# Experts of a mixture layer: tokens stationary instead of weights, spare rows as fp32 products on four column groups

## What is computed

```python
def grouped_moe(x, router_w, router_bias, w1, w3, w2):
    ...
    _, top_idx = lax.top_k(masked_sel, TOP_K)          # 2 of 16 experts, within one group of 4
    ...
    for e in range(N_EXPERTS):
        h = jax.nn.silu(t @ w1[e]) * (t @ w3[e])       # 1024 -> 512, twice
        y = y + gate[:, e:e + 1] * (h @ w2[e])         # 512 -> 1024
    return y.reshape(Bsz, S, D)
```

## Time and profile before

| | us |
|---|---|
| median of 3 runs | 1072.06 |
| lowest and highest | 1067.51, 1075.02 |
| the profiled execution, its own time | 1075.18 |
| its span in the trace | 1073.5 |

### The profile page before, as it was taken

The page is one execution under the profiler, slowest core; times in us unless marked ns, Lnnn a source line. Parts: engine busy times, 40 slices in busy tenths (PEclk is TensorE's granted clock), DMA queues, the critical chain, the costliest instruction groups (busy, mean ns, idle before and its releaser), DMA issues.

```text
span 1073.5 us, 17120 instructions
## 1 busy us (share of the span) xinstructions
PE 976.4 (91%) x6074; PEld 838.3 (78%) x6074; DVE 679.5 (63%) x1042; ACT 527.3 (49%) x894; POOL 242.1 (23%) x258
## 2 busy tenths in 40 slices
PE   6998999989999999799993898999999999999950
PEld 5777998976777777588883787888888888888840
DVE  3202723655546745865558776888888888888727
ACT  3212512224545645631122665777777777777524
POOL 2000000000000000100001847444444443543216
PEclk9998999998999999899995898999999999999985
DMA  9201020001101301296326798999999999999236
GB/s 253 45 20 40 20 79 21 1 2 51 28 21 40 70 1 40 90 274 261 115 95 179 182 285 225 277 285 285 286 285 285 284 286 277 301 278 289 68 88 254
DMA packets 200643, 168.12 MB, mean 157 GB/s; under 512 B 26992, under 2 KB 179568, under 8 KB 200592
## 3 DMA queue, kind: packets, MB, share of 16 engines
q1 hardware_dynamic: 187072, 145.05, 47.2%
q0 software_dynamic: 10480, 21.20, 8.4%
q10 hardware_dynamic: 3040, 1.19, 0.5%
HBM read 142.87 MB, written 24.54 MB: 156 GB/s over the span
## 4 chain that ended last, share of the span: by engine, by line
PE 80%; DVE 7%; DMA 4%; ACT 4%; POOL 3%; issue 3%; SPq 0%; POOLq 0%; DVEq 0%; ACTq 0%
PE pz L954 15%; PE bank L655 12%; PE bank L657 12%; PE bank L656 12%; PE pz L956 6%; PE pz L813 2%; PE pz L981 2%; PE pz L979 2%; PE bank L826 2%; PE bank L840 2%; PE bank L903 1%; PE pz L656 1%; PE pz L657 1%; PE pz L655 1%; PE bank L937 1%
## 5 line engine op out<-in xcount | busy, mean ns | idle before, releaser
L954 PE MATMUL pz<-xT,eh 128*128 128x320 f32 x1024 | 267.9, 349 | 4.2 <-DVE yB L1638 3.3
L1511 DVE TENSOR_TENSOR el<-er,eh 128x1024 fp32r<-128x1024 f32 x192 | 230.1, 1222 | 29.8 <-ACT eh L1207 27.8
L956 PE MATMUL pz<-xT,el 128*128 128x160 f32 x1024 | 243.2, 238 | 0.0
L954 PEld LDWEIGHTS pz<-xT,eh 128*128 128x128 f32 x1024 | 194.5, 190 | 6.6 <-issue 3.5
L956 PEld LDWEIGHTS pz<-xT,el 128*128 128x128 f32 x1024 | 198.2, 194 | 0.7
L1207 ACT ACTIVATE eh<-er 128x1024 fp32r<-128x1024 f32 x192 | 196.5, 1051 | 0.4
L1444 DVE TENSOR_TENSOR_SCAN Qs<-Qs 128x128 f32<-128x128 f32 (+7 forms) x48 | 65.0, 1354 | 78.9 <-ACT Qs L1125 78.9
L655 PE MATMUL bank<-xT_hi,w_hi 128*128 128x512 f32 x256 | 105.8, 413 | 3.3 <-DVE xT_lo L1328 3.3
L657 PE MATMUL bank<-xT_hi,w_lo 128*128 128x512 f32 x256 | 101.6, 397 | 0.0
L656 PE MATMUL bank<-xT_lo,w_hi 128*128 128x512 f32 x256 | 101.2, 395 | 0.0
L530 POOL IOTA zidl<- 112x160 uint32 x1 | 0.3, 298 | 439.7 <-ACT aT L1136 439.7
(11 more groups left out here) (260 smaller groups left out, 1861.3 us busy)
## 6 DMA issues: line engine op xcount, KB each, us to landing
er<-in_w_dram SPq DMA_DIRECT2D x192, 512.0 KB, 7.0
w_raw<-in_w_in_dram SPq DMA_DIRECT2D x21, 512.0 KB, 3.8
x_row<-in_x_dram SPq DMA_DIRECT2D x8, 512.0 KB, 9.1
xres<-in_x_dram SPq DMA_DIRECT2D x8, 512.0 KB, 5.4
x_scratch<-x SPq DMA_DIRECT2D x8, 512.0 KB, 2.7
sum_scratch<-x SPq DMA_DIRECT2D x8, 512.0 KB, 4.1
cx<-sum_scratch SPq DMA_DIRECT2D x8, 512.0 KB, 7.1
out_dram<-cx SPq DMA_DIRECT2D x8, 512.0 KB, 2.6
```

Of the source, the lines that this page charges most:

```text
L954: pe.matmul(bank, eh[:, p, ks], xT2[:, k, :, :].rearrange("p a t -> p (a t)"), start=(k == 0), stop=False, skip_group_check=True)
L956: last = pe.matmul(bank[:, 0:TW], el[:, p, ks], xT2[:, k, 0, :], start=False, stop=(k == NK - 1), skip_group_check=True)
L1511: dve.tensor_tensor(el[:, p, :], er[:, p, :], eh[:, p, :].bitcast(F32), ALU.subtract).then_inc(S["el_ok"], 1)
```

## The change

**Gate and up.** Now the tokens are stationary and the weights pass, 512 columns at a time: `rows_gu` calls `mm3` for gate and for up, 8 slices each, into the banks gA and uA (128 tokens x 512). The spare rows leave this path: `spare_gu` multiplies them in raw fp32, from `er` and the unsplit transposed rows `xB`, each slice as four products of 32 stationary and 128 passing columns, that write to four groups of 32 partitions of one bank (column groups of the array). The pieces of w1 and w3 are now two slices of 128 rows by all 512 outputs; in DRAM their contiguous runs are 2048 bytes instead of 512.

**Hidden rows.** silu and product are made once for the 128 main rows (`silA`, `hA`, 128 x 512) and once for the spare rows (`silB`, `hB`, 128 x 128, four quarters of the outputs in four partition groups). As tokens now lie on partitions, both are transposed on TensorE (one and four more transposes), and `hA` is split into `hTh` and `hTl`. The copies and sums of cross terms go.

**Down.** The main rows as before, by `mm3`. The spare rows in raw fp32, 4 x 4 products of 32 stationary and 256 passing columns, into four partition groups, ahead of the main rows. `yB` is thus 128 x 256, quarter rows, which are added into the sums viewed as quarter rows, ahead of `yA`.

**Pieces.** A piece of `er` comes free when both its low half and its raw products (`raw_done`) are done. AHEAD is 4, and pieces 4 to 11 are split in the block that uses them.

**Tables.** The token numbers and gates of a block are loaded once into one of four tables, `tab` and `tabQ`, instead of twice; `gates` copies the gates out. The loop takes four blocks a turn. The first block starts when the transposed spare rows are there, and its rounds of transposes have these first.

The core of the diff; of the functions that are written anew only the new lines stand here (the old ones are printed above), and names of semaphores, small buffers and the waits of `piece_hi` are left out.

```diff
--- before.py
+++ after.py
-AHEAD = 6
+AHEAD = NF
...
+        tab = [small(f"tab{r}", [P, 4], U32) for r in range(4)]
+        tabQ = [small(f"tabQ{r}", [P, 1], U32) for r in range(4)]
+        slotG = small("slotG", [P, 2])
...
+        gA, uA = pz[0][:, 0:512], pz[0][:, 512:1024]
+        guB = pz[1][:, 0:2 * P]
+        hTA_bank = pz[0][:, 0:512].rearrange("p (f t) -> p f t", f=NF)
+        hTB_bank = pz[1][:, 2 * P:3 * P].rearrange("p (f s) -> p f s", f=NF)
+        yB_bank = pz[1][:, 512:512 + DQ]
...
+                    sp.wait_ge(S["raw_done"], NPIECE * b - NPIECE + p + 1)
+                dst = er[:, p:p + 1, :]
                 if p < 2 * NF:
-                    src = (w1v, w3v)[p % 2][:, bass.ds(e, 1), :, (p // 2) * P:(p // 2 + 1) * P]
-                    dst = er[:, p:p + 1, :].rearrange("p e (k f) -> p e k f", k=NK)
+                    src = (w1v, w3v)[p // NF][:, bass.ds(e, 1), 2 * (p % NF):2 * (p % NF) + 2, :]
+                    dst = dst.rearrange("p e (k f) -> p e k f", k=2)
                 else:
                     src = w2v[:, bass.ds(e, 1), p - 2 * NF, :]
-                    dst = er[:, p:p + 1, :]
                 sp.dma_start(dst, src).then_inc(S[f"e_in{p}"], 16)
...
+            def load_table(r, b):
+                if not (isinstance(b, int) and b < 4):
+                    pool.wait_ge(S["y_out"], 32 * (b - 3))
+                    pool.sem_inc(S["pool_go"], 1)
+                pool.dma_start(tab[r][:, 0:2], idl_dram[bass.ds(b * TW, P), :]).then_inc(S["idx_in"], 16)
+                for g in range(NQ):
+                    pool.dma_start(tab[r][g * TR:(g + 1) * TR, 2:4], idl_dram[bass.ds(b * TW + P, TR), :]).then_inc(S["idx_in"], 16)
+            def quarters(r, b, loaded=1):
+                pool.wait_ge(S["idx_in"], 16 * (1 + NQ) * (b + loaded))
                 pool.sem_inc(S["pool_go"], 1)
...
+                pool.tensor_scalar(tabQ[r][:, :], tab[r][:, 2:3], float(NQ), quad[:, 0:1], ALU.mult, ALU.add).then_inc(S["idxq_ok"], 1)
+            def gather(r, b):
+                pool.wait_ge(S["idxq_ok"], b + 1)
                 pool.wait_ge(S["xtr_ps"], NXR * b)
                 pool.sem_inc(S["pool_go"], 1)
...
+                pool.indirect_dma_start(xgA[:, :], None, x1_dram, bass.IndirectOffsetOnAxis(tab[r][:, 0:1], 0)).then_inc(S["xg_in"], 16)
+                pool.indirect_dma_start(xgB[:, :], None, x1_quarters, bass.IndirectOffsetOnAxis(tabQ[r][:, 0:1], 0)).then_inc(S["xg_in"], 16)
+            def gates(r, b):
+                pool.tensor_copy(slotG[:, :], tab[r][:, 1:4:2].bitcast(F32)).then_inc(S["slot_ok"], 1)
+            def add_rows(r, b):
+                pool.wait_ge(S["slot_ok"], b + 1)
+                pool.wait_ge(S["yB_ev"], b + 1)
+                pool.sem_inc(S["pool_go"], 1)
+                if first_block(b):
+                    pool.tensor_scalar(yB[:, :], yB[:, :], slotG[:, 1:2], None, ALU.mult).then_inc(S["y_gated"], 1)
+                    pool.wait_ge(S["y_gated"], 1)
+                pool.indirect_dma_start(sum_quarters, bass.IndirectOffsetOnAxis(tabQ[r][:, 0:1], 0), yB[:, :], None, compute_op=ALU.add)\
+                    .then_inc(S["y_out"], 16)
...
+            def step(r, b):
+                load_table(r, b)
+                gates((r + 2) % 4, b - 2)
+                quarters(r, b)
+                gather(r, b)
+                add_rows((r + 2) % 4, b - 2)
...
+                b0 = NE * j
+                for e in range(3):
+                    load_table(e, b0 + e)
+                for e in range(3):
+                    quarters(e, b0 + e, 3 - e)
+                    if e == 2 or not isinstance(j, int):
+                        gather(e, b0 + e)
+                gates(0, b0)
+                add_rows(0, b0)
+                step(3, b0 + 3)
+                with pool.Fori(1, NE // 4) as i:
+                    for u in range(4):
+                        step(u, b0 + 4 * i + u)
+                for e in (NE - 2, NE - 1):
+                    gates(e % 4, b0 + e)
+                    add_rows(e % 4, b0 + e)
...
+            def spare_gu(b):
+                for p in range(2 * NF):
+                    pe.wait_ge(S[f"e_in{p}"], 16 * b + 16)
+                    m = p // NF
+                    for h in range(2):
+                        k = 2 * (p % NF) + h
+                        for g in range(NQ):
+                            last = pe.matmul(guB[g * TR:(g + 1) * TR, m * P:(m + 1) * P], xB[:, k, :],
+                                             er[:, p, h * 512 + g * P:h * 512 + (g + 1) * P],
+                                             start=(k == 0), stop=(k == NK - 1), skip_group_check=True)
+                    last.then_inc(S["raw_done"], 1)
...
+            def rows_gu(b, m):
+                for p in range(NF * m, NF * m + NF):
+                    pe.wait_ge(S["el_ok"], NPIECE * b + p + 1)
+                    for h in range(2):
+                        k = 2 * (p - NF * m) + h
+                        last = mm3(pe, (gA, uA)[m], 0, NK - 1, lambda k: (xh[:, k, :], xl[:, k, :]),
+                                   lambda k: (k_of(eh, p, h), k_of(el, p, h)), [k])
+                    last.then_inc(S["piece_done"], 1)
...
             def pe_block(b, nxt):
...
+                pe.wait_ge(S["xTh_ok"], NXR * b + (1 if first_block(b) else NXR))
+                spare_gu(b)
+                pe.wait_ge(S["xTl_ok"], 2 * b + 2)
+                rows_gu(b, 0)
+                rows_gu(b, 1)
+                pe.wait_ge(S["hB_ok"], b + 1)
+                pe.transpose(pz[1][:, 2 * P:3 * P], hB[:, :], ident[:, :]).then_inc(S["hTB_ps"], 1)
                 if nxt:
                     x_transposes(b + 1, (0, 1))
+                pe.wait_ge(S["hA_ok"], b + 1)
+                for f in range(NF):
+                    last = pe.transpose(gA[:, f * P:(f + 1) * P], hA[:, f * P:(f + 1) * P], ident[:, :])
+                last.then_inc(S["hTA_ps"], 1)
+                if nxt:
+                    x_transposes(b + 1, (2,))
+                pe.wait_ge(S["hTB_ok"], b + 1)
+                if not first_block(b):
+                    pe.wait_ge(S["yB_ev"], b)
+                for f in range(NF):
+                    p = 2 * NF + f
+                    pe.wait_ge(S[f"e_in{p}"], 16 * b + 16)
+                    for g in range(NQ):
+                        last = pe.matmul(yB_bank[g * TR:(g + 1) * TR, :], hTB[:, f, :], er[:, p, g * DQ:(g + 1) * DQ],
+                                         start=(f == 0), stop=(f == NF - 1), skip_group_check=True)
+                    last.then_inc(S["raw_done"], 1)
+                pe.wait_ge(S["hTl_ok"], b + 1)
                 if not first_block(b):
                     pe.wait_ge(S["yA0_ev"], b)
                     pe.wait_ge(S["yA1_ev"], b)
                 for f in range(NF):
...
+                    p = 2 * NF + f
+                    pe.wait_ge(S["el_ok"], NPIECE * b + p + 1)
                     for half in range(2):
...
+                        last = mm3(pe, pp[half][:, :], 0, NF - 1, lambda f: (hTh[:, f, :], hTl[:, f, :]),
+                                   lambda f: (k_of(eh, p, half), k_of(el, p, half)), [f])
                         if f == NF - 1:
                             last.then_inc(S["rowsA_ps"], 1)
...
+                        elif half:
+                            last.then_inc(S["piece_done"], 1)
...
+                x_transposes(NE * j, ROUNDS_FIRST)
...
+                piece_hi(b, 4)
+                piece_hi(b, 5)
+                act.wait_ge(S["raw_done"], NPIECE * b + 2 * NF)
+                act.activation(silB[:, :], guB[:, 0:P], ACT.Silu).then_inc(S["silB_ok"], 1)
+                for p in range(6, 10):
+                    piece_hi(b, p)
+                act.wait_ge(S["piece_done"], (NPIECE - 1) * b + NF)
+                act.activation(silA[:, :], gA, ACT.Silu).then_inc(S["silA_ok"], 1)
+                piece_hi(b, 10)
+                piece_hi(b, 11)
+                act.wait_ge(S["hTB_ps"], b + 1)
+                act.activation(hTB[:, :, :], hTB_bank, ACT.Copy).then_inc(S["hTB_ok"], 1)
                 if nxt:
...
+                    x_hi(b + 1, (0,))
+                act.wait_ge(S["hTA_ps"], b + 1)
+                act.activation(hTh[:, :, :], hTA_bank, ACT.Copy).then_inc(S["hTh_ok"], 1)
+                if nxt:
+                    x_hi(b + 1, (1, 2))
+                    piece_hi(b + 1, 0)
+                act.wait_ge(S["raw_done"], NPIECE * b + NPIECE)
                 if not first_block(b):
                     act.wait_ge(S["y_out"], 32 * b)
...
+                    act.wait_ge(S["slot_ok"], b + 1)
+                act.activation(yB[:, :], yB_bank, ACT.Copy, scale=1.0 if first_block(b) else slotG[:, 1:2])\
+                    .then_inc(S["yB_ev"], 1)
                 if nxt:
...
+                    for p in range(1, 4):
                         piece_hi(b + 1, p)
...
+                act.wait_ge(S["rowsA_ps"], 2 * b + 2)
```

(26 more changed lines are left out.)

232 lines of the change are left out of this document (45 added, 187 removed).

## The result

| | before, us | after, us |
|---|---|---|
| median of 4 runs | 1073.32 | 1032.20 |
| lowest and highest | 1067.51, 1075.02 | 1030.00, 1035.04 |
| profiled execution, its own time | 1075.18 | 1031.45 |
| its span | 1073.5 | 1029.6 |

The ratio is 0.9624, with a 95% interval of 0.9595 to 0.9653: 41 us less. The forecast was 1032.

What follows compares the result with a forecast made beforehand. TensorE's matmuls were taken to bound each block: 23.55 us instead of 26.67. With block 3 at 686.2, twelve such blocks, the last block and the tail gave 40.6 us less, 1032 against the 1072.06 median; range 1015 to 1062.

Steps and rivals of the forecast that it cites:

- TensorE's sum per block: Steady expert block: TensorE's matmuls, transposes and changes between parts add up to 23.55 us against 26.67 before.
- the four changes between whole array and column groups: TensorE, each block: at most one 0.11 us drain each, at least nothing; taken as 0.3 us together.
- The unknown price: Spare fp32 products on four column groups: four for the price of one, 3.5 us gate/up and 1.73 down a block.
- Rival A: Spare products: fp32 column groups run only two at a time, 10.5 us instead of 5.2, block 28.8, total 1103; chance 0.07.
- the issue rival: Spare products: halves start no closer than 0.055 us, gate/up 7.0 us, block 27.1, total 1078; chance 0.04.
- no start closer than about 25 ns: TensorE, spare products: by this skill rule the 160 halves want 4.0 us a block and the sum stays.
- Rival C: Stalls at the joints in every block (hA late, yB's bank held), 2 us a block, total 1058; chance 0.09.
- The transfers: DMA per block: 21.2 us, under TensorE's 23.55; if longer runs gain nothing, 24.9, total 1050, a rival with chance 0.13.
- The first blocks: Blocks 0 to 2: GpSimd decides, they gain almost nothing, block 3 starts at 686.2 against 688.55.
- a start before 680: Sign: block 3 starting before 680 or after 692 would show the reading of the first blocks wrong.
- A gather that stays where it was: Block 1's gather on GpSimd: unmoved, so TensorE's transposes for block 1 wait until 614.84 as before.
- The stall that the prediction put at 3 us in block 2: Block 2: ScalarE waits for GpSimd's multiplications and adds before going on, making hA late by 3 us.

Runs made afterwards that it cites:

- e1: Changed kernel with the gate/up spare products issued one column group after the other instead of in turn; 1151.47 us in one run.
- e2: Changed kernel without the 80 fp32 products of the spare rows (gate/up and down); 980.84 us in one run.
- e7: Changed kernel with each gate/up piece loaded by four transfers of 128 columns, so runs are 512 bytes again; 1045.49 us, ratio 0.9764.
- e9: Changed kernel run once more, nothing edited, for its profile; 1027.36 us.
- e11: Kernel before run once more, nothing edited, for its profile; 1067.47 us.
- e5: Changed kernel with block 1's gather ahead of both scatters, and these held until TensorE has started block 0's gate/up spare products; 1029.17 us.
- e10: Changed kernel with two table loads ahead of block 2's gather instead of three, block 1's coming behind block 0's adds; 1030.17 us.

## Why the prediction was right

**TensorE's sum per block.** Forecast 23.55, measured 23.93. The term that was sized wrong is the one for the four changes between whole array and column groups. The prediction took 0.3 for them together, and one 0.11 each as the most. The other terms add up to 23.24, so they cost 0.69, 0.17 each. On the way into the column groups 0.32 us lie between two starts instead of 0.23; on the way out the last step of four halves is 0.11 longer, and the first matmul of 512 columns has 0.34 to the next (706.41 to 706.75 above). These delays are why each part is a little over its forecast, the main down matmuls for instance 5.67 and not 5.47. A block is 0.38 over its forecast; over twelve blocks that is 4.6 us.

**The unknown price.** The reading of L813, L826 and L924 together was right: four on four groups for the price of one. Rival A (two at a time) and the issue rival, each start no closer than L826's 0.055, are refuted by four starts within 20 ns and the next four 0.109 us later, and e1 shows what that overlap is worth. The rule from the Trainium skill that was weighed (TensorE: Matmul & The Clock Gate, section "Wait — 56ns, not 53.3ns?"), no start closer than about 25 ns, doesn't hold across column groups: the starts within a step are 6 to 7 ns apart. Its 62 ns for each matmul that the microcode handles would have made the spare products 9.9 us; they take 5.5.

**What TensorE hides.** VectorE 17.40 and ScalarE 15.65 in a block (18.4 and 17 forecast); the splits keep ahead and the handovers are covered, the one of hTl because the spare down products stand in front (e2 waits 1.3 us there without them). Rival C, stalls at the joints, therefore came true in no steady block.

**The transfers.** 21.2 us forecast as their bound, at most 20.7 by e2; 24.9 without longer runs, 25.3 by e7. The mean rate of the steady blocks rose from 272 to 317 GB/s, and the packets went from 106061 to 40494:

```profile
DMA packets 40494, 91.09 MB, mean 317 GB/s; under 512 B 4826, under 2 KB 6362, under 8 KB 40493
```

**The first blocks: this step failed.** The prediction said that they "gain almost nothing", with block 3 at 686.2, and that a start before 680 would prove the reading wrong. It was 678.84, and 675.33 in e9. Part of that is the base: the profile of before had its experts late, by 5.7 us against e11, which has nothing to do with the step. Counted from the first transposes, to be free of it, blocks 0 to 2 were forecast at 98.3 us; they took 94.0 and 90.9, against 100.6 and 98.4 before. What failed is the chain of GpSimd up to block 2's gather, whose times the prediction had carried over unchanged from one profile of the kernel before. All times here are us after the first transposes:

| | before | before, e11 | forecast | after, with gaps | after, e9 |
|---|---|---|---|---|---|
| block 1's gather issued | 14.9 | 13.8 | 14.9 | 12.7 | 13.8 |
| block 1's transposes | 26.9 | 26.1 | 26.9 | 36.9 | 23.4 |
| first table or slot load | 37.8 | 33.4 | 37.8 | 27.4 | 30.5 |
| block 2's gather issued | 49.0 | 43.7 | 53.1 | 39.5 | 46.1 |
| block 2's transposes | 56.9 | 54.5 | 61.0 | 60.9 | 51.5 |
| block 3 starts | 100.6 | 98.4 | 98.3 | 94.0 | 90.9 |

The forecast against e9, which has no gaps either: the tables start 7.3 us sooner, from there to the gather it takes 15.6 (15.2 forecast), and its rows are transposed 5.4 us after its issue instead of 7.9. That puts block 2's transposes 9.4 us ahead. TensorE then needs 9.2 us to block 2 and not 10.8, since the clock stayed at 1.00 behind the short wait. Block 2 itself gives 3.6 of this back: 30.1 us where 26.5 were forecast. Together that is 7.4 us.

Of the 7.3 us of the tables, 4.4 lie between the two executions of the kernel before and so belong to the base; 2.9 lie between e11 and e9. "A gather that stays where it was" is right for its issue, 13.8 us in both, and wrong for its landing: the transposes follow 8.3 us after its second half was issued in e9, and 10.7 and 11.1 before. Why it lands sooner, no run tells.

The scatters themselves are part of the spread. GpSimd's timeline before and after, one scatter each beside a busy VectorE and beside an idle one; first the kernel before:

```profile
597.01 1.96 POOL L555 DMA_INDIRECT slot_tokens<-tokg,rows_u  x1 [0.30 <-issue]
```

and the kernel after, in the gaps of block 0:

```profile
602.76 0.98 POOL L569 DMA_INDIRECT slot_tokens<-tokg,rows_u  x1 [0.30 <-issue]
```

All 16 with the gather between them took 28.0 us before (26.8 in e11) and 24.0 after (26.1 in e9), and GpSimd waited 8.5 us (5.4) for their data to land before, 2.1 (3.0) after. The large difference of the first pair, in which VectorE stood still for 20 us, is thus not what the change does without gaps.

The stall that the prediction put at 3 us in block 2 came true in e9 and was 6.2 us, against a steady block; in the first profile it was absent, as block 0's gaps had left GpSimd time to add.

**How the errors met.** The forecast put block 3 7.4 us too late (3.1 because the experts started earlier, 4.3 by the step above); that and 4.6 too few saved in the steady blocks leave block 15 2.8 early, and from there to the loads it took 0.4 longer than forecast: the loads of the final norm at 997.90 against 1000.3. The time of 1032 is right to 0.2 us by some luck: for the profiled execution the forecast was 1034.6 and the measured time 1031.45, and the difference is as large as the experts' earlier start. The range of 1015 to 1062 and the shape of the sum were right by the working.

## What to carry to other kernels

Write products for different column groups in turn, never one group's after another's: the order alone was worth 7.6 us a block here. When TensorE's work shrinks, ask at once what the transfers would need, since a block that wanted 26.67 could hide 512-byte runs and one of 23.93 could not. A single profile is no base for a start-up phase: measure it in several executions of both kernels, and count from an event inside the phase.

## What was not expected of the hardware

TensorE can fall into gaps of 0.3 to 1.0 us after each few instructions, with no releaser, for some 20 us; the same program had them in one execution and not in another. They came only while GpSimd's small scatters were written or had just been, but the six other profiled runs with these products (e5 to e10) had the scatters without gaps. The cause stays open.

An indirect scatter of GpSimd took 0.98 to 1.04 us wherever VectorE was idle for its whole length, in all profiles here, and between 0.98 and 2.02 beside a working VectorE. The two stand side by side in the traces; no run changed VectorE's work to test it.

The DMA share says little on how much room is left: 0.97 at 314 GB/s (the changed kernel) and 1.01 at 350 GB/s (e2) are the same transfers in 23.93 and 20.65 us a block.

Each change of TensorE between the whole array and column groups costs some 0.17 us here, the way out more than the way in.
